# Feature-major tiles with each low-weight product between two high-weight ones

## The chip, the cores and the metric

The kernel runs on one core of one Trainium2 chip. The time is the device time of one execution in microseconds; before the change the median of 3 runs is 2253.44 us (2252.5 to 2256.35). The engines of the core work side by side: TensorE multiplies matrices (PE in the profile, and PEld for the load of its stationary operand), VectorE (DVE) and ScalarE (ACT) do elementwise work, SyncE (SP) issues the transfers.

## The reference

Two transformer blocks follow one another over 256 tokens of width 2048, all in float32. Nearly all of the arithmetic is in products of the activations with weight matrices: an input projection, an output projection, an up-projection and a down-projection in each block.

```python
h = rms_norm(x, pre_mix_norm[l])
proj = h @ w_in[l]                      # queries, keys, values, gates
...
x = x + rms_norm(mix @ w_out[l], post_mix_norm[l])
h = rms_norm(x, pre_ffn_norm[l])
u = causal_dwconv(h @ w_up[l], conv_w[l], conv_b[l])
gate, up = jnp.split(u, 2, axis=-1)
y = (jax.nn.gelu(gate, approximate=True) * up) @ w_down[l]
x = x + rms_norm(y, post_ffn_norm[l])
```

The second block has the same frame with another attention, a recurrent branch and an up-projection without the convolution.

## The kernel before

**Weights.** Every weight matrix passes through the core once, in tiles of 128 x 1024 float32 (512 KB). SyncE loads them into eight slots of `stage`. ScalarE copies a tile to `whi` in the matmul's reduced float32 format (L786 for the up-projections), and VectorE writes what that copy lost, stage - whi, to `wlo` (L1220). Both have four slots (`SPLITS`). The activations are kept in the same way: in `actT[:, k, :]` columns 0 to 255 hold the high parts of 256 tokens for chunk k of 128 input features, and columns 256 to 511 the low parts. A product in float32 is then hi x hi + lo x hi + hi x lo, three products in the reduced format.

**Feature-major tiles** give an output with features on the partitions: the weights are the stationary operand, the activations stream. A tile holds 4 chunks (`FC`) of 256 features, in two halves f = 0, 1 of 128. For a chunk and a half there is one high-weight product, whi against all 512 columns, into the whole of PSUM bank f, and one low-weight product, wlo against the 256 high columns, added to columns 256 to 511 of the same bank. So a chunk has the high products of both halves and then the low products of both halves. Four tiles of 4 chunks run over the 2048 input features and fill two banks. Such tiles stand in three places with the same body: `feat` for the up-projections (L2018, L2022, in a loop on the engine), `in1_tile` for the first block's input projection (L2090, L2093), and `in2_tile` for the second's (L2361, L2364).

**Token-major tiles** (`tok`, `tok_tile`) have the activations as stationary operand and stream the weights, 512 columns wide in most, 256 or 280 in a few; three products a chunk and half of the tokens (L1905 to L1907; L2106 to L2108; L2374 to L2376). They aren't touched.

**What sets the order.** TensorE's program is written out by hand and runs in that order. At its first load a tile waits for `lo_done` (VectorE has written its wlo), and its last product increments `tile_used`. ScalarE waits for that before it writes over the slot of four tiles ago. SyncE refills a `stage` slot once VectorE has read it. In the first block after a norm (`turned`), each chunk also waits for `actlo_...`, its activations' low part.

Of the kernel before, what the change touches and what calls it, by code (L numbers as in the profile page):

```python
# [16 lines left out]
P = 128  # L17
D = 2048
S = 256
TT = S // P  # L20
KC = D // P
# [29 lines left out]
SPLITS = 4  # L51
# [4 lines left out]
FW = 256  # L56
FC = TILE // FW
FT = 2 * KC // FC
# [50 lines left out]
def in1_block(n):  # L109

    k = max(k for k in range(len(IN1_BLOCKS)) if IN1_FIRST[k] <= n)
    return k, n - IN1_FIRST[k]
# [13 lines left out]
def in2_block(n):  # L126

    k = max(k for k in range(len(IN2_BLOCKS)) if IN2_FIRST[k] <= n)
    return k, n - IN2_FIRST[k]
# [74 lines left out]
def build(nc, w, out, scratch, roots):  # L204
# [4 lines left out]
    def ev(name):  # L209

        if name not in sems:
            sems[name] = ctx.enter_context(nc.semaphore(name))
        return sems[name]

    with ctx:
        def sb(name, shape, dt=F32, on=ctx):
            return on.enter_context(nc.sbuf_tensor(name, shape, dt))
# [3 lines left out]
        whi = sb("whi", [P, SPLITS, TILE], F32R)  # L221
        wlo = sb("wlo", [P, SPLITS, TILE], F32R)
# [15 lines left out]
        actT = sb("actT", [P, KC, 2 * S], F32R, here)  # L238
# [88 lines left out]
        PS = ctx.enter_context(nc.psum_tensor("PS", [P, 8, 512], F32))  # L327
# [1572 lines left out]
        def _(pe):  # L1900
# [47 lines left out]
            def last_chunks(turn):  # L1948

                n = {"n2": 0, "n3": 1, "n4": 2}[turn]  # L1950
                pe.wait_ge(ev("actlo_" + turn), 4)
                turn_chunks(turn, range(12, KC))
                pe.wait_ge(ev("resid"), PIECES * n + 6)
                turn_chunks(turn, range(12, KC), t=1)
# [43 lines left out]
            def feat(name, down=None, turned=None):  # L1998

                g = G[name]  # L2000

                def one(i, s):
                    new = turned is not None and isinstance(i, int) and i == 0
                    pe.wait_ge(ev("pre_done"), i + (g.acc + 1))
                    if s == 1 and down is not None:
                        pe.wait_ge(ev("acc_free"), 2 + G[down].acc + G[down].blocks)
                    for j in range(FT):
                        if new and j == 1:
                            last_chunks(turned)
                        pe.wait_ge(ev("lo_done"), i * FT + (g.first + j + 1 + STAGES))  # L2010
                        for c in range(FC):
                            k = j % (FT // 2) * FC + c
                            if new and j < FT // 2:
                                pe.wait_ge(ev("actlo_" + turned), k + 1)
                            for f in range(2):
                                o = PS[:, 4 * (s ^ g.turned) + 2 * (j // (FT // 2)) + f, :]
                                at = slice(c * FW + f * P, c * FW + (f + 1) * P)
                                nc.tensor.matmul(o, whi[:, j % SPLITS, at], actT[:, k, :], start=k == 0, stop=False)  # L2018
                            for f in range(2):
                                o = PS[:, 4 * (s ^ g.turned) + 2 * (j // (FT // 2)) + f, :]  # L2020
                                at = slice(c * FW + f * P, c * FW + (f + 1) * P)
                                last = nc.tensor.matmul(o[:, S:2 * S], wlo[:, j % SPLITS, at], actT[:, k, 0:S],  # L2022
                                                        start=False, stop=k == KC - 1)
                        last.then_inc(ev("tile_used"), 1)
                if turned is not None:
                    one(0, 0)
                    one(1, 1)
                with pe.Fori(1 if turned is not None else 0, g.blocks // 2) as r:
                    for s in range(2):
                        one(r * 2 + s, s)  # L2030

            def turn(name, ready, n):

# [38 lines left out]
            def in1_tile(n):  # L2072

                k, j = in1_block(n)
                kind, _, wd = IN1_BLOCKS[k]
                bank, s = 2 * (k % 2), n % SPLITS
                if k == 0:
                    pe.wait_ge(ev("actlo_n1"), FC * (j + 1))
                elif j == 0 and k >= 2:
                    if k - 2 in IN1_FEAT:  # L2080
                        pe.wait_ge(ev("in1_join"), IN1_FEAT[k - 2] + 1)
                    else:
                        pe.wait_ge(ev("in1_tok"), 2 * IN1_TOK[k - 2] + 2)
                pe.wait_ge(ev("lo_done"), n + 1 + STAGES)
                if kind == "feat":
                    for c in range(FC):
                        at_k = FC * j + c
                        for f in range(2):
                            o, at = PS[:, bank + f, :], slice(c * FW + f * P, c * FW + (f + 1) * P)
                            nc.tensor.matmul(o, whi[:, s, at], actT[:, at_k, :], start=at_k == 0, stop=False)  # L2090
                        for f in range(2):
                            o, at = PS[:, bank + f, :], slice(c * FW + f * P, c * FW + (f + 1) * P)
                            last = nc.tensor.matmul(o[:, S:2 * S], wlo[:, s, at], actT[:, at_k, 0:S], start=False, stop=at_k == KC - 1)  # L2093
                else:
                    last = tok_tile(bank, s, wd, TC * j)
                last.then_inc(ev("tile_used"), 1)
# [240 lines left out]
            def in2_tile(n):  # L2337

                k, j = in2_block(n)
                kind, _, wd = IN2_BLOCKS[k]  # L2340
                banks, s = IN2_BANKS[k], n % SPLITS
                if j == 0 and k == 14:
                    pe.wait_ge(ev("in2_join"), FEAT_NO[12] + 1)
                elif j == 0 and k > 14:
                    pe.wait_ge(ev("in2_tok"), 2 * TOK_NO[k - 2] + 2)
                elif k < 14 and j == 0 and k >= 2:
                    if k - 2 in FEAT_NO:
                        pe.wait_ge(ev("in2_join"), FEAT_NO[k - 2] + 1)
                    else:
                        pe.wait_ge(ev("in2_tok"), 2 * TOK_NO[k - 2] + 2)  # L2350
                if k == 0 and j == 2:
                    last_chunks("n3")
                if k == 0:
                    pe.wait_ge(ev("actlo_n3"), TC * (j + 1))
                pe.wait_ge(ev("lo_done"), G["in2"].first + n + 1 + STAGES)
                if kind == "feat":
                    for c in range(FC):
                        at_k = FC * j + c
                        for f in range(2):
                            o, at = PS[:, banks[f], :], slice(c * FW + f * P, c * FW + (f + 1) * P)  # L2360
                            nc.tensor.matmul(o, whi[:, s, at], actT[:, at_k, :], start=at_k == 0, stop=False)  # L2361
                        for f in range(2):
                            o, at = PS[:, banks[f], :], slice(c * FW + f * P, c * FW + (f + 1) * P)
                            last = nc.tensor.matmul(o[:, S:2 * S], wlo[:, s, at], actT[:, at_k, 0:S], start=False, stop=at_k == KC - 1)  # L2364
                else:
                    for t in range(TT):
                        if t == 1 and j == 0 and k >= 14:
                            pe.wait_ge(ev("in2_tok"), 2 * TOK_NO[k - 1] + 1)
                        for c in range(TC):
                            at_k = TC * j + c  # L2370
                            h, l = whi[:, s, c * wd:(c + 1) * wd], wlo[:, s, c * wd:(c + 1) * wd]
                            o = PS[:, banks[t], 0:wd]
                            ah, al = actT[:, at_k, t * P:(t + 1) * P], actT[:, at_k, S + t * P:S + (t + 1) * P]
                            nc.tensor.matmul(o, ah, h, start=at_k == 0, stop=False)  # L2374
                            nc.tensor.matmul(o, ah, l, start=False, stop=False)  # L2375
                            last = nc.tensor.matmul(o, al, h, start=False, stop=at_k == KC - 1)  # L2376
                        if t == 0 and j == 7 and k >= 13:
                            last.then_inc(ev("first_half"), 1)
                last.then_inc(ev("tile_used"), 1)
# [183 lines left out]
```

## Time and profile before

| | |
|---|---|
| median of 3 runs | 2253.44 us (2252.5 to 2256.35) |
| profiled execution, first to last instruction | 2250.0 us |
| its own time beyond the span | not listed; the median of the runs is 3.44 us above the span |
| TensorE, matmuls | 2225.6 us, 99% |
| TensorE, weight loads | 1890.7 us, 84% |
| VectorE | 1415.9 us, 63% |
| ScalarE | 1117.9 us, 50% |
| mean HBM and DMA rate | 186 GB/s |

Matmuls are pipelined, and the end of each is modelled by the profiler, so a record is longer than the time until the next one starts, and records overlap. The busy time of TensorE therefore says only that it never stands still for long, not that it works at its peak.

### The profile page before, as it was taken

How to read it: one execution, taken by the hardware profiler on the slowest of the kernel's cores; microseconds unless marked ns; L12 is line 12 of the kernel's file. 1: busy time of each engine (PE TensorE's matmuls, PEld its weight loads, DVE VectorE, ACT ScalarE, POOL GpSimd, SP SyncE). 2: the span in 40 equal slices, each digit the busy share in tenths (PEclk: the TensorE clock that was granted, in tenths of full speed). 3: DMA queues.
4: the chain of work that ended last, by engine and by line, in shares of the span. 5: the costliest groups of instructions: out<-in, count | busy, mean ns of one | idle time of the engine just before them, and what ended most of it. 6: DMA issues, size and time to landing. Idle time of an engine off the chain costs nothing.

```text
span 2250.0 us, 34148 instructions
## 1 busy us (share of the span) xinstructions
PE 2225.6 (99%) x12721; PEld 1890.7 (84%) x12721; DVE 1415.9 (63%) x1826; ACT 1117.9 (50%) x1566; POOL 65.6 (3%) x95
## 2 busy tenths in 40 slices
PE   8999999999999999999999999999999999999998
PEld 7888888888888888888888888888888888888886
DVE  5567685677776447777566786656665444666545
ACT  5454464555555445555454554545444344444443
POOL 4100000000000000000000000000000000000000
PEclk9999999999999999999999999999999999999999
DMA  9954455566566666656657455566666666666663
GB/s 286 312 182 135 132 168 178 157 192 204 177 199 193 189 193 188 186 187 199 205 147 204 141 165 156 181 194 170 189 193 189 191 191 190 192 187 189 213 188 111
DMA packets 321663, 418.84 MB, mean 186 GB/s; under 512 B 13566, under 2 KB 233048, under 8 KB 320788
## 3 DMA queue, kind: packets, MB, share of 16 engines
q1 hardware_dynamic: 316548, 398.81, 58.4%
q0 software_dynamic: 4720, 16.49, 2.5%
q10 hardware_dynamic: 288, 2.10, 0.2%
q8 instruction: 69, 1.13, 0.2%
q14 instruction: 38, 0.31, 0.0%
HBM read 414.85 MB, written 2.49 MB: 185 GB/s over the span
## 4 chain that ended last, share of the span: by engine, by line
PE 93%; DVE 3%; DMA 2%; ACT 1%; issue 1%; POOL 0%; SPq 0%; POOLq 0%; DVEq 0%; ACTq 0%
PE PS L2018 24%; PE PS L2022 12%; PE PS L1907 10%; PE PS L1906 10%; PE PS L1905 10%; PE PS L2090 5%; PE PS L2361 3%; PE PS L2093 2%; PE PS L2106 2%; PE PS L2108 2%; PE PS L2107 2%; PE PS L2364 2%; PE PS L2374 1%; PE PS L2376 1%; PE PS L2375 1%; DMA root_rows<-small 1%
## 5 line engine op out<-in xcount | busy, mean ns | idle before, releaser
L2018 PE MATMUL PS<-actT,whi 128*128 128x512 f32 x2432 | 759.1, 393 | 0.2 <-DVE wlo L1220 0.2
L2022 PEld LDWEIGHTS PS<-actT,wlo 128*128 128x128 f32 x2432 | 457.2, 188 | 103.5
L1220 DVE TENSOR_TENSOR wlo<-stage,whi 128x1024 fp32r<-128x1024 f32 x296 | 360.2, 1223 | 220.4 <-ACT whi L786 220.1
L1192 DVE TENSOR_TENSOR wlo<-stage,whi 128x1024 fp32r<-128x1024 f32 x245 | 299.1, 1226 | 307.3 <-ACT whi L728 307.3
L2022 PE MATMUL PS<-actT,wlo 128*128 128x256 f32 x2432 | 479.5, 279 | 0.0
L786 ACT ACTIVATE whi<-stage 128x1024 fp32r<-128x1024 f32 x296 | 311.6, 1058 | 308.1 <-PE PS L2022 294.6
L728 ACT ACTIVATE whi<-stage 128x1024 fp32r<-128x1024 f32 x245 | 258.6, 1058 | 351.1 <-PE PS L1907 327.5
L2018 PEld LDWEIGHTS PS<-actT,whi 128*128 128x128 f32 x2432 | 366.3, 188 | 0.9 <-issue 0.4
L1907 PE MATMUL PS<-whi,gT 128*128 128x512 f32 x864 | 340.4, 394 | 0.0
L1906 PE MATMUL PS<-wlo,gT 128*128 128x512 f32 x864 | 338.7, 392 | 0.0
L1905 PE MATMUL PS<-whi,gT 128*128 128x512 f32 x864 | 335.2, 388 | 0.0
L1623 DVE TENSOR_TENSOR wlo<-stage,whi 128x1024 fp32r<-128x1024 f32 (+2 forms) x125 | 145.4, 1166 | 110.0 <-ACT whi L977 109.7
L977 ACT ACTIVATE whi<-stage 128x1024 fp32r<-128x1024 f32 (+2 forms) x125 | 125.7, 1008 | 150.2 <-PE PS L2093 80.7
L1906 PEld LDWEIGHTS PS<-wlo,gT 128*128 128x128 f32 x864 | 162.2, 188 | 37.8
L1905 PEld LDWEIGHTS PS<-whi,gT 128*128 128x128 f32 x864 | 162.2, 188 | 36.1
L1907 PEld LDWEIGHTS PS<-whi,gT 128*128 128x128 f32 x864 | 162.4, 188 | 32.2
L2090 PE MATMUL PS<-actT,whi 128*128 128x512 f32 x512 | 163.5, 400 | 1.2 <-DVE wlo L1404 1.2
L1831 DVE TENSOR_TENSOR wlo<-stage,whi 128x1024 fp32r<-128x1024 f32 (+1 forms) x86 | 102.9, 1203 | 62.7 <-ACT whi L1128 62.2
L1128 ACT ACTIVATE whi<-stage 128x1024 fp32r<-128x1024 f32 (+1 forms) x86 | 89.3, 1044 | 90.2 <-PE PS L2364 45.3
L2361 PE MATMUL PS<-actT,whi 128*128 128x512 f32 x384 | 121.7, 398 | 0.7 <-DVE wlo L1831 0.7
L2093 PEld LDWEIGHTS PS<-actT,wlo 128*128 128x128 f32 x512 | 96.2, 188 | 22.0
L2093 PE MATMUL PS<-actT,wlo 128*128 128x256 f32 x512 | 101.1, 279 | 0.0
(334 smaller groups left out, 2479.3 us busy)
## 6 DMA issues: line engine op xcount, KB each, us to landing
stage<-in_w_up SPq DMA_DIRECT2D x304, 512.0 KB, 4.0
stage<-in_w_down SPq DMA_DIRECT2D x216, 512.0 KB, 4.2
stage<-in_w_in SPq DMA_DIRECT2D x160, 512.0 KB, 3.8
stage<-in_w_out SPq DMA_DIRECT2D x64, 512.0 KB, 4.1
stage<-in_w_in SPq DMA_DIRECT2D x16, 256.0 KB, 3.3
DQK<-in_cmp_k_w POOLq DMA_DIRECT2D x8, 512.0 KB, 7.4
DQK<-in_cmp_v_w POOLq DMA_DIRECT2D x8, 512.0 KB, 7.3
stage<-in_w_in SPq DMA_DIRECT2D x8, 280.0 KB, 8.1
```

The lines of the kernel that those rows point to most:

```text
L728: nc.scalar.activation(whi[:, s % SPLITS, 0:wd], stage[:, s % STAGES, 0:wd], ACT.Copy)\
L786: nc.scalar.activation(whi[:, j % SPLITS, :], stage[:, j, :], ACT.Copy).then_inc(ev("hi_done"), 1)
L1192: nc.vector.tensor_tensor(wlo[:, s % SPLITS, 0:wd], stage[:, s % STAGES, 0:wd], whi[:, s % SPLITS, 0:wd].bitcast(F32), ALU.subtract).then_ ...
L1220: nc.vector.tensor_tensor(wlo[:, j % SPLITS, :], stage[:, j, :], whi[:, j % SPLITS, :].bitcast(F32), ALU.subtract).then_inc(ev("lo_done"), 1)
L1905: nc.tensor.matmul(o, ah, h, start=k == 0, stop=False)
L1906: nc.tensor.matmul(o, ah, l, start=False, stop=False)
L1907: return nc.tensor.matmul(o, al, h, start=False, stop=ends and c == TC - 1)
L2018: nc.tensor.matmul(o, whi[:, j % SPLITS, at], actT[:, k, :], start=k == 0, stop=False)
L2022: last = nc.tensor.matmul(o[:, S:2 * S], wlo[:, j % SPLITS, at], actT[:, k, 0:S], start=False, stop=k == KC - 1)
L2090: nc.tensor.matmul(o, whi[:, s, at], actT[:, at_k, :], start=at_k == 0, stop=False)
L2093: last = nc.tensor.matmul(o[:, S:2 * S], wlo[:, s, at], actT[:, at_k, 0:S], start=False, stop=at_k == KC - 1)
L2361: nc.tensor.matmul(o, whi[:, s, at], actT[:, at_k, :], start=at_k == 0, stop=False)
```

## The change

The three bodies of a feature-major tile are replaced by one function, `feat_tile`. It issues the same sixteen products in another order: the low product of the second half is held back by one chunk and put between the two high products of the next chunk, and the low product of the first half follows the second high product. At the end of a tile the last low product that was held back is issued.

```diff
+            def feat_tile(bank, s, k0, before_chunk=None):
+
+                def high(f, c):
+                    at = slice(c * FW + f * P, c * FW + (f + 1) * P)
+                    nc.tensor.matmul(PS[:, bank + f, :], whi[:, s, at], actT[:, k0 + c, :], start=k0 + c == 0, stop=False)
+
+                def low(f, c):
+                    at = slice(c * FW + f * P, c * FW + (f + 1) * P)
+                    return nc.tensor.matmul(PS[:, bank + f, S:2 * S], wlo[:, s, at], actT[:, k0 + c, 0:S],
+                                            start=False, stop=k0 + c == KC - 1)
+
+                for c in range(FC):
+                    if before_chunk is not None:
+                        before_chunk(k0 + c)
+                    high(0, c)
+                    if c:
+                        low(1, c - 1)
+                    high(1, c)
+                    low(0, c)
+                return low(1, FC - 1)
...
                 if kind == "feat":
-                    for c in range(FC):
-                        at_k = FC * j + c
-                        for f in range(2):
-                            o, at = PS[:, bank + f, :], slice(c * FW + f * P, c * FW + (f + 1) * P)
-                            nc.tensor.matmul(o, whi[:, s, at], actT[:, at_k, :], start=at_k == 0, stop=False)
-                        for f in range(2):
-                            o, at = PS[:, bank + f, :], slice(c * FW + f * P, c * FW + (f + 1) * P)
-                            last = nc.tensor.matmul(o[:, S:2 * S], wlo[:, s, at], actT[:, at_k, 0:S], start=False, stop=at_k == KC - 1)
+                    last = feat_tile(bank, s, FC * j)
```

In `feat` and `in2_tile` the same body is replaced by the same call. In `feat` the wait for a chunk's activations is passed as `before_chunk`.

TensorE, one tile of the up-projections in the engine's loop, before. L2018 is a high product, L2022 a low one, and L2010 computes the value of the wait at a tile's start.

```order
L2010 REGISTER_ALU
L2018 MATMUL PS<-actT,whi 128x512 x2
L2022 MATMUL PS<-actT,wlo 128x256 x2
L2018 MATMUL PS<-actT,whi 128x512 x2
L2022 MATMUL PS<-actT,wlo 128x256 x2
L2018 MATMUL PS<-actT,whi 128x512 x2
L2022 MATMUL PS<-actT,wlo 128x256 x2
L2018 MATMUL PS<-actT,whi 128x512 x2
L2022 MATMUL PS<-actT,wlo 128x256 x2
L2010 REGISTER_ALU
```

The products stand in pairs of two highs and two lows. The same engine with the change, from the third chunk of such a tile over its end into the next one; L2028 is now the high product, L2032 the low one.

```order
L2028 MATMUL PS<-actT,whi 128x512
L2032 MATMUL PS<-actT,wlo 128x256
L2028 MATMUL PS<-actT,whi 128x512
L2032 MATMUL PS<-actT,wlo 128x256
L2028 MATMUL PS<-actT,whi 128x512
L2032 MATMUL PS<-actT,wlo 128x256 x2
L2010 REGISTER_ALU
L2028 MATMUL PS<-actT,whi 128x512 x2
L2032 MATMUL PS<-actT,wlo 128x256
L2028 MATMUL PS<-actT,whi 128x512
L2032 MATMUL PS<-actT,wlo 128x256
L2028 MATMUL PS<-actT,whi 128x512
```

Inside a tile high and low products take turns; one pair of lows is left at its end and one pair of highs at its start. The programs of the other engines have the same instructions in the same order as before.

## Rows read from the trace of the kernel before

**Rows 1.** The page: busy us (share) x instructions; clock in 40 slices; chain by engine.
```profile
PE 2225.6 (99%) x12721; PEld 1890.7 (84%) x12721; DVE 1415.9 (63%) x1826; ACT 1117.9 (50%) x1566; POOL 65.6 (3%) x95
...
PEclk9999999999999999999999999999999999999999
...
PE 93%; DVE 3%; DMA 2%; ACT 1%; issue 1%; POOL 0%; SPq 0%; POOLq 0%; DVEq 0%; ACTq 0%
```

**Rows 2.** The page's groups: shapes, count, busy us, mean ns, idle us before, its releaser.
```profile
L2018 PE MATMUL PS<-actT,whi 128*128 128x512 f32 x2432 | 759.1, 393 | 0.2 <-DVE wlo L1220 0.2
...
L786 ACT ACTIVATE whi<-stage 128x1024 fp32r<-128x1024 f32 x296 | 311.6, 1058 | 308.1 <-PE PS L2022 294.6
...
L2090 PE MATMUL PS<-actT,whi 128*128 128x512 f32 x512 | 163.5, 400 | 1.2 <-DVE wlo L1404 1.2
...
L2361 PE MATMUL PS<-actT,whi 128*128 128x512 f32 x384 | 121.7, 398 | 0.7 <-DVE wlo L1831 0.7
```

**Rows 3.** Stretches: length, busy us per engine, granted clock, DMA share, GB/s.
```profile
428.00:822.00 394.00, 393.85 (x2093) 338.00 (x2091) 258.17 (x300) 205.24 (x244) 3.38 (x4) 1.00 0.62 191
```

**Rows 4.** Timeline of TensorE, up-projection: start us, us; eight chunks apart.
```profile
1700.00 0.39 PE L2018 MATMUL PS<-actT,whi 128*128 128x512 f32 x1
...
1705.55 0.39 PE L2018 MATMUL PS<-actT,whi 128*128 128x512 f32 x1
```

**Rows 5.** Single products of one chunk, in order: min/median/max ns, first and last start.
```profile
L2018 PE MATMUL PS<-actT,whi x1: 388/388/388, 1700.0 to 1700.0; 128*128 128x512 f32 x1
...
L2018 PE MATMUL PS<-actT,whi x1: 398/398/398, 1700.2 to 1700.2; 128*128 128x512 f32 x1
...
L2022 PE MATMUL PS<-actT,wlo x1: 281/281/281, 1700.5 to 1700.5; 128*128 128x256 f32 x1
...
L2022 PE MATMUL PS<-actT,wlo x1: 276/276/276, 1700.6 to 1700.6; 128*128 128x256 f32 x1
```

**Rows 6.** Single products of a token-major chunk, same columns.
```profile
L1905 PE MATMUL PS<-whi,gT x1: 388/388/388, 700.0 to 700.0; 128*128 128x512 f32 x1
...
L1906 PE MATMUL PS<-wlo,gT x1: 392/392/392, 700.3 to 700.3; 128*128 128x512 f32 x1
...
L1907 PE MATMUL PS<-whi,gT x1: 394/394/394, 700.5 to 700.5; 128*128 128x512 f32 x1
```

**Rows 7.** Timeline of TensorE, token-major: five triples apart.
```profile
700.04 0.39 PE L1905 MATMUL PS<-whi,gT 128*128 128x512 f32 x1
...
703.47 0.39 PE L1905 MATMUL PS<-whi,gT 128*128 128x512 f32 x1
```

**Rows 8.** Waits of TensorE on its high products: us in total, times, longest.
```profile
PE PS L2018 <- DVE wlo L1220: 0.2, 1, 0.2
```

**Rows 9.** Single 512-column products: after 512; after 256 token-major; after a stall; after low.
```profile
L2018 PE MATMUL PS<-actT,whi x1: 394/394/394, 824.3 to 824.3; 128*128 128x512 f32 x1
...
L2361 PE MATMUL PS<-actT,whi x1: 394/394/394, 1174.9 to 1174.9; 128*128 128x512 f32 x1
...
L2107 PE MATMUL PS<-wlo,actT x1: 396/396/396, 171.2 to 171.2; 128*128 128x512 f32 x1
...
L1905 PE MATMUL PS<-whi,gT x1: 390/390/390, 692.5 to 692.5; 128*128 128x512 f32 x1
```

**Rows 10.** Groups of 256-column token-major products, 66 to 70 and 73 to 77 us.
```profile
L2108 PE MATMUL PS<-whi,actT 128*128 128x256 f32 x13 | 3.6, 276 | 0.0
...
L2106 PE MATMUL PS<-whi,actT 128*128 128x256 f32 x12 | 3.4, 280 | 0.0
L2108 PE MATMUL PS<-whi,actT 128*128 128x256 f32 x12 | 3.3, 279 | 0.0
L2107 PE MATMUL PS<-wlo,actT 128*128 128x256 f32 x12 | 3.3, 279 | 0.0
```

**Rows 11.** Weight loads of the high products, 1700 to 1800 us: min/median/max ns.
```profile
L2018 PEld LDWEIGHTS PS<-actT,whi x36: 187/188/188, 1699.9 to 1711.8; 128*128 128x128 f32 x36
```

More of the change, by code:

```diff
@@ L2010, in one, with chunk_split @@
                         pe.wait_ge(ev("lo_done"), i * FT + (g.first + j + 1 + STAGES))
-                        for c in range(FC):
-                            k = j % (FT // 2) * FC + c
+                        def chunk_split(k):
                             if new and j < FT // 2:
                                 pe.wait_ge(ev("actlo_" + turned), k + 1)
-                            for f in range(2):
-                                o = PS[:, 4 * (s ^ g.turned) + 2 * (j // (FT // 2)) + f, :]
-                                at = slice(c * FW + f * P, c * FW + (f + 1) * P)
-                                nc.tensor.matmul(o, whi[:, j % SPLITS, at], actT[:, k, :], start=k == 0, stop=False)
-                            for f in range(2):
[L2020 to L2024, printed above, removed]
+                        feat_tile(4 * (s ^ g.turned) + 2 * (j // (FT // 2)), j % SPLITS, j % (FT // 2) * FC, chunk_split)\
+                            .then_inc(ev("tile_used"), 1)
                 if turned is not None:
@@ L2085, in in1_tile @@
                 if kind == "feat":
-                    for c in range(FC):
-                        at_k = FC * j + c
-                        for f in range(2):
-                            o, at = PS[:, bank + f, :], slice(c * FW + f * P, c * FW + (f + 1) * P)
-                            nc.tensor.matmul(o, whi[:, s, at], actT[:, at_k, :], start=at_k == 0, stop=False)
-                        for f in range(2):
-                            o, at = PS[:, bank + f, :], slice(c * FW + f * P, c * FW + (f + 1) * P)
-                            last = nc.tensor.matmul(o[:, S:2 * S], wlo[:, s, at], actT[:, at_k, 0:S], start=False, stop=at_k == KC - 1)
+                    last = feat_tile(bank, s, FC * j)
                 else:
@@ L2356, in in2_tile @@
                 if kind == "feat":
[L2357 to L2364, printed above, removed]
+                    last = feat_tile(banks[0], s, FC * j)
                 else:
```

## Prediction

> **What bounds the kernel now.** I read the page first. TensorE is busy for 99% of the span, its clock row stands at 9 in every slice, and the chain of waits lies on it for 93% [rows 1]. VectorE and ScalarE, which cut the weight tiles into a high and a low part, spend their idle time waiting for TensorE to free a slot (ScalarE's whi copy of L786: 308.1 us idle, 294.6 of it released by L2022) [rows 2]. In the stretch that holds the first up-projection, 428 to 822 us, the DMA engines are used to 0.62 and TensorE is busy for 393.85 of 394 us [rows 3]. So no transfer and no other engine is near the path there: what a chunk of matmuls costs TensorE is what the kernel costs.
>
> Then I went down to single instructions. Feature-major tiles have 2432 + 512 + 384 high-weight products (L2018, L2090, L2361) [rows 2]. A tile has eight, so there are 3328 / 8 = 416 tiles, of 4 chunks of two high (512 columns) and two low (256 columns). In the timeline the first high product of a chunk starts at 1700.00 and the same one eight chunks on at 1705.55 [rows 4]: 5.55 / 8 = 694 ns a chunk, 2.775 us a tile, and 416 tiles x 2.775 = 1154 us, half of the kernel. At the full clock (granted 1.00 in rows 3, the 2.4 GHz level) 1536 columns would stream in 640 ns. 54 ns a chunk, 416 x 4 x 54 = 90 us in all, are thus not column time. They are all that an order of the same sixteen matmuls can win back.
>
> Recorded durations tell how far one start lies from the next. The four of a chunk last 388, 398, 281 and 276 ns [rows 5]; their sum is 1343, the pitch 694, so each record is (1343 - 694) / 4 = 162 ns longer than its pitch. Token-major tiles confirm the 162: 388 + 392 + 394 = 1174 [rows 6] against five triples from 700.04 to 703.47, 686 ns each [rows 7]; (1174 - 686) / 3 = 163. I therefore use differences of records as differences of pitch. What the reader should see in rows 5 is that the two high products of a chunk differ by 10 ns, and the two low ones by 5, although the two are the same instruction with another bank and other weights.
>
> **What the change does.** It adds and removes no instruction. Per tile there are again 8 high and 8 low products, as many weight loads, one wait for lo_done at the tile's first load and one increment at its last product; banks, slots and SP's and the converters' programs stay. What moves is the neighbourhood. Before, each chunk was H H L L, so of eight highs four came after a low and four after a high. Now a tile is H H L H L H L H L H L H L H L L. Of the highs one is first (after the last tile's low, before a high), one second (after a high, before a low), and six stand between two lows; of the lows six stand between two highs, and the last two are as before. At a tile's end the product whose end frees the slot is still the last one, so nobody gets a buffer earlier or later within a tile. In the first blocks after a norm, a chunk's wait for its activations (actlo) now also stands ahead of the last low product of the chunk before. That concerns 16 chunks of two calls, and TensorE's waits list only 0.2 us at L2018 [rows 8]; I take it as nothing, and if each such product stood exposed it would be 30 x 0.12 = 3.6 us.
>
> The whole effect is therefore the price of a high between lows and of a low between highs. The trace of before has neither. I bound them by the nearest rows: the high at 388 or 398, the low at 276 or 281 [rows 5]. Both at the low end give 6 x (393 - 388) + 6 x (278.5 - 276) = 45 ns a tile below before (a tile's averages are 393 and 278.5), 416 x 0.045 = 18.7 us; both at the high end give 18.7 us more.
>
> Which end depends on what makes rows 5 differ, the product ahead or the one behind.
> If it is the **product ahead** (the state in which it leaves the array and the load path), a high after a low costs 388 and a low after a high 281. Per tile: 6 x (388 - 393) = -30, 6 x (281 - 278.5) = +15, sum -15 ns. 416 x -0.015 = -6.2 us.
> For it: a high after a high, with a high behind it too, is found once at the border from a token-major block, 394 [rows 9]; with a low ahead the same product is 388 [rows 5]. So 6 of the 10 ns come with the product ahead. The second product after a stall has no low near it, and reads 396 [rows 9].
> Against it: a high after a token-major low-width product reads 394 [rows 9], not 388, and the 256-column products of token-major tiles run at 276 in one stretch and at 279 to 280 in another, with the same neighbours [rows 10]. So more than the neighbour counts.
>
> I take -6.2 us, because three of the four comparisons that rows 9 allow go with the product ahead or do not speak against it (the fourth: a token-major high after a low is 390, within the 388 to 394 of its kind [rows 6, 9]).
>
> Here a rule of the Trainium skill speaks against the change. The load of a low product's successor has only the low product to hide under: load records last 188 ns and begin with the matmul ahead [rows 11], while a low product's pitch is 276 - 162 = 114 to 119 ns. "TensorE: Matmul & The Clock Gate", section "LDWEIGHTS (loading the stationary operand)", says that a load takes its columns divided by 1.2 GHz, an estimate of 107 ns for 128 columns, and its part 2 that loads are pulled ahead under the running matmul. By that there is one load under every product in either order, and the sum would be nothing, 2253.4 us.
>
> **Rivals.**
> B, the **costs add up, whatever the order**. In token-major tiles a high averages (388 + 392 + 394) / 3 = 391.3, and a 256-column product at its slower pitch 279.3 [rows 6, 10]; 2 x 391.3 + 2 x 279.3 = 1341 against the 1343 of a chunk. Or, read in two parts, 6 ns of a high come from ahead and 4 from behind (388, 394, 398), so a high between lows is 392, and a low 276 to 281: per tile 6 x (392 - 393) + 6 x (-2.5 to +2.5) = -21 to +9 ns, -8.7 to +3.7 us, middle -2.5, time 2250.9 us. For it: the sum fits to 2 ns. Against it: such a fit is no proof while 256-column products have two pitches.
>
> C, **slower: the product behind sets the pitch**, because its weights load during it. A high with a low behind it then costs 398, a low with a high behind it 276. Per tile 6 x (398 - 393) + 6 x (276 - 278.5) = +15 ns, 416 x 0.015 = +6.2 us, time 2259.6 us. The place is each of the six inner high products of every tile, and it decides once more than half of the 10 ns in rows 5 is owed to the wlo load that follows. For it: the rows 5 that carry A carry C equally well, as ahead and behind change together there. Against it: the 394 and 396 of rows 9, slow highs with no low behind them.
>
> That the change does nothing that it says is excluded by the order of the program: the rows of the section on the change show each low product between two high ones.
>
> **The numbers.** The profiled execution has a span of 2250.0 us, and the median of the runs is 3.4 above it; the difference lies outside the span and is left as it is. 2253.44 - 6.2 = 2247.2 us. About 0.2%, 4.5 us, is what a measurement of this kernel can tell from no change. A has 0.42, and would be seen as faster. B has 0.33: 0.05 faster, 0.25 same, 0.03 slower. C has 0.25: 0.22 slower, 0.03 same. Faster 0.47, same 0.28, slower 0.25. The range goes from 2240 (between A and the bound of -18.7) to 2261 (C with the small waits of the first blocks partly exposed); beyond it at either end lies a tenth. A's own range is 2241 (inner highs at 388 and inner lows at their old average: 30 ns a tile, -12.5 us) to 2250.
>
> **What would show it.** For A: in the profile after, eight chunks of an inner stretch take about 5.52 us instead of 5.55 (15 ns a tile), the inner highs read 388 and the inner lows 281, the share of DMA rises by less than 0.01 and the waits stay as they are. For B: highs near 392 and lows near 278. For C: highs at 398, lows at 276. All fail if the inner pair falls into a rhythm of its own, below 276 or above 398, or if a wait for wlo appears at the tile starts. Token-major tiles must stay at 388, 392, 394; if they move, something outside these tiles is at work.

## The result and the profile after

The changed kernel takes 2270.15 us (median of 4 runs, 2269.3 to 2270.91) against 2253.43 us (4 runs): ratio 1.0075, 95% interval 1.0057 to 1.0093. It is slower by 16.7 us where 6.2 us faster was forecast, and lies above the range's upper end of 2261.

One correction to the time before: each run lists its span beside its time, and the time is 1.8 us longer (2270.44 against 2268.6 us here, 2251.94 against 2250.1 us in a run of the kernel before). So of the 3.44 us that the section on the time before puts beyond the span, some 1.6 us are that its three runs were slower than the profiled execution. That is also most of why the medians differ by 16.7 us and the spans by 18.6.

The page and a stretch of 400 us from the first up-projection into the down-projection behind it:

```profile
span 2268.6 us, 34148 instructions
...
PE 2244.2 (99%) x12721; PEld 1899.7 (84%) x12721; DVE 1416.8 (62%) x1826; ACT 1119.4 (49%) x1566; POOL 65.8 (3%) x95
...
L2028 PE MATMUL PS<-actT,whi 128*128 128x512 f32 x3328 | 1148.1, 398 | 1.9 <-DVE wlo L1404 1.3
L2032 PE MATMUL PS<-actT,wlo 128*128 128x256 f32 x3328 | 867.7, 281 | 0.0
...
L786 ACT ACTIVATE whi<-stage 128x1024 fp32r<-128x1024 f32 x296 | 312.9, 1058 | 322.4 <-PE PS L2032 308.9
```

```profile
432.00:832.00 400.00, 400.00 (x2099) 341.61 (x2098) 258.93 (x300) 207.17 (x245) 3.39 (x4) 1.00 0.62 189
```

Counts, clock and DMA share are those of before [rows 1 to 3], no new wait has come up (1.9 us in all at L2028, as much as at the three lines before), and ScalarE idles 14 us longer for TensorE [rows 2]. The span has grown by 18.6 us, on TensorE. L2028 and L2032 now stand for all three places. The mean record of a high product there is 398 ns; before, the three lines give (2432 x 393 + 512 x 400 + 384 x 398) / 3328 = 395 [rows 2]. A low one reads 281 on average, and 279 before. So the time is in the pitch of the moved products, that is, in the time from one start to the next. The timeline from the inside of one tile to the end of the next (start us, us):

```profile
1709.99 0.40 PE L2028 MATMUL PS<-actT,whi 128*128 128x512 f32 x1
1710.22 0.28 PE L2032 MATMUL PS<-actT,wlo 128*128 128x256 f32 x1
1710.34 0.40 PE L2028 MATMUL PS<-actT,whi 128*128 128x512 f32 x1
1710.58 0.28 PE L2032 MATMUL PS<-actT,wlo 128*128 128x256 f32 x1
1710.69 0.40 PE L2028 MATMUL PS<-actT,whi 128*128 128x512 f32 x1
1710.93 0.40 PE L2032 MATMUL PS<-actT,wlo 128*128 128x256 f32 x2
1711.17 0.39 PE L2028 MATMUL PS<-actT,whi 128*128 128x512 f32 x1
...
1713.99 0.63 PE L2028 MATMUL PS<-actT,whi 128*128 128x512 f32 x2
```

A pair of high and low takes 0.35 us (1709.99, 1710.34, 1710.69), and a tile 1713.99 - 1711.17 = 2.82 us. Over forty tiles the starts are

```profile
1926.45 0.63 PE L2028 MATMUL PS<-actT,whi 128*128 128x512 f32 x2
...
2039.25 0.63 PE L2028 MATMUL PS<-actT,whi 128*128 128x512 f32 x2
```

so 112.80 / 40 = 2.820 us a tile. Before, the same forty tiles start at

```profile
1910.46 0.62 PE L2018 MATMUL PS<-actT,whi 128*128 128x512 f32 x2
...
2021.40 0.62 PE L2018 MATMUL PS<-actT,whi 128*128 128x512 f32 x2
```

and take 110.94 / 40 = 2.773 us each. 416 tiles x 0.0467 = 19.4 us, slightly more than the span's 18.6: not every tile runs at the steady pitch, and in the first up-projection forty tiles of the kernel before take 2.784 us each. The single records (min/median/max ns) that answer to rows 5:

```profile
L2028 PE MATMUL PS<-actT,whi x1: 398/398/398, 1710.0 to 1710.0; 128*128 128x512 f32 x1
...
L2032 PE MATMUL PS<-actT,wlo x1: 281/281/281, 1710.2 to 1710.2; 128*128 128x256 f32 x1
...
L2028 PE MATMUL PS<-actT,whi x1: 394/394/394, 1708.3 to 1708.3; 128*128 128x512 f32 x1
```

Between two lows the high reads 397 to 398 (but for the first of the six in a tile, 392), between two highs the low reads 281 to 283: each takes the dearer of its two values in rows 5. A pair is (398 - 162) + (281 - 162), nearly 354 ns; from the forty tiles' starts it is 353.3, against 346.7 as the mean of before. The two highs at a tile's start, 394 each (the last row), add up to 788 ns, where 388 and 398 were 786.

### The profile page after: what moved, and what is told of

Same layout as the page of the kernel before. It is cut to its first block, busy times and chain, and to the rows that moved or that the text cites. A ratio compares the mean times of both kernels' runs of the same rounds, so it can differ in the third digit from the quotient of the medians.

```text
span 2268.6 us, 34148 instructions
## 1 busy us (share of the span) xinstructions
PE 2244.2 (99%) x12721; PEld 1899.7 (84%) x12721; DVE 1416.8 (62%) x1826; ACT 1119.4 (49%) x1566; POOL 65.8 (3%) x95
## 4 chain that ended last, share of the span: by engine, by line
PE 95%; DVE 2%; DMA 1%; ACT 1%; issue 1%; POOL 0%; SPq 0%; POOLq 0%; DVEq 0%; ACTq 0%
PE PS L2028 33%; PE PS L2032 17%; PE PS L1906 10%; PE PS L1905 10%; PE PS L1907 10%; PE PS L2112 2%; PE PS L2114 2%; PE PS L2113 2%; PE PS L2373 1%; PE PS L2375 1%; PE PS L2374 1%; DVE x L1354 1%; DMA root_rows<-small 1%; PE PS L2143 0%; PE PS L2236 0%
## 5 line engine op out<-in xcount | busy, mean ns | idle before, releaser
L2028 PE MATMUL PS<-actT,whi 128*128 128x512 f32 x3328 | 1148.1, 398 | 1.9 <-DVE wlo L1404 1.3
L2032 PE MATMUL PS<-actT,wlo 128*128 128x256 f32 x3328 | 867.7, 281 | 0.0
L2028 PEld LDWEIGHTS PS<-actT,whi 128*128 128x128 f32 x3328 | 596.2, 188 | 123.1 <-issue 6.1
L2032 PEld LDWEIGHTS PS<-actT,wlo 128*128 128x128 f32 x3328 | 624.6, 188 | 37.9
L1220 DVE TENSOR_TENSOR wlo<-stage,whi 128x1024 fp32r<-128x1024 f32 x296 | 360.5, 1224 | 234.7 <-ACT whi L786 234.4
L1906 PE MATMUL PS<-wlo,gT 128*128 128x512 f32 x864 | 340.4, 394 | 0.0
L1905 PE MATMUL PS<-whi,gT 128*128 128x512 f32 x864 | 338.7, 392 | 0.0
L1907 PE MATMUL PS<-whi,gT 128*128 128x512 f32 x864 | 335.3, 388 | 0.0
L1905 PEld LDWEIGHTS PS<-whi,gT 128*128 128x128 f32 x864 | 162.2, 188 | 37.8
L1907 PEld LDWEIGHTS PS<-whi,gT 128*128 128x128 f32 x864 | 162.2, 188 | 36.3
L1906 PEld LDWEIGHTS PS<-wlo,gT 128*128 128x128 f32 x864 | 162.4, 188 | 32.1
L1243 DVE SCALAR_TENSOR_TENSOR grow<-pre,convT,grow 128x256 f32<-128x256 f32 x176 | 73.6, 481 | 31.7 <-ACT grow L801 29.0
L2112 PE MATMUL PS<-whi,actT 128*128 128x512 f32 (+2 forms) x240 | 88.9, 371 | 0.0
L2114 PE MATMUL PS<-whi,actT 128*128 128x512 f32 (+2 forms) x240 | 87.1, 363 | 0.0
L2113 PE MATMUL PS<-wlo,actT 128*128 128x512 f32 (+2 forms) x240 | 86.8, 362 | 0.0
```

The source lines that it names most:

```text
L1220: nc.vector.tensor_tensor(wlo[:, j % SPLITS, :], stage[:, j, :], whi[:, j % SPLITS, :].bitcast(F32), ALU.subtract).then_inc(ev("lo_done"), 1)
L1905: nc.tensor.matmul(o, ah, h, start=k == 0, stop=False)
L1907: return nc.tensor.matmul(o, al, h, start=False, stop=ends and c == TC - 1)
L2028: nc.tensor.matmul(PS[:, bank + f, :], whi[:, s, at], actT[:, k0 + c, :], start=k0 + c == 0, stop=False)
L2032: return nc.tensor.matmul(PS[:, bank + f, S:2 * S], wlo[:, s, at], actT[:, k0 + c, 0:S], start=False, stop=k0 + c == KC - 1)
```

## The experiments

All numbers of tile pitch below are from starts some 32 to 40 tiles apart in one up-projection. Each run's ratio is to runs of the kernel before on the same chip (medians of 2251.9 to 2255.0 us). First, which neighbourhood costs: four other orders of the same sixteen products, and later e7, a fifth. In the expectations of e1 to e4, rival B is the bank and rival C the chunk; they aren't the rivals B and C of the prediction.

```diff
 e1: per chunk        high(0, c); low(0, c); high(1, c); low(1, c)
 e2: per chunk        high(0, c); low(0, c - 1); high(1, c); low(1, c - 1); two lows at the end
 e3: per two chunks   four highs, then four lows
 e4: per tile         eight highs (0, 1, 0, 1, ...), then eight lows
 e7: per tile         high(0, 0..3), high(1, 0..3), then the lows likewise
```

> Order H0 L0 H1 L1 of the same chunk: widths alternate as in the changed kernel, but a low product follows the high one of its own bank and of its own chunk, and the next high goes to the other bank. Theory W (a product costs more when its neighbours have the other width; 15 ns of TensorE time for each pair of changes high-low and low-high, from 45 ns a tile for three more such pairs): 8 pairs a tile where before had 4, so 60 ns a tile over before, 416 x 0.060 = 25 us, about 2278 us; inner highs recorded at 397, lows at 281. Rival B (the high that follows a low writes into the bank that the low has just written): that is gone here, 2253 us. Rival C (the stream changes its chunk of activations at nearly every product): half gone here, about 2262 us.

> Both low products stand one chunk behind: H0(c) L0(c-1) H1(c) L1(c-1). Banks as in e1 (a low follows a high of the same bank, the next high changes bank), but every product streams another chunk than the one ahead of it. Theory W: a tile is H0 H1 first, then alternates, and ends on two lows, as in the changed kernel, 7 pairs, about 2270 us. Rival B (bank of the next high): 2253 us. Rival C (chunk changes at each product): 2270 us or more, and clearly above e1.

> Two chunks at a time: four highs, then four lows. Theory W: 2 pairs of width changes a tile instead of 4, 30 ns a tile less than before, 416 x 0.030 = 12.5 us, about 2241 us. Rivals B and C: the banks change at each product as before, and the chunk changes no more often: 2253 us. If a high costs 229 and a low 118 wherever neighbours are equal (the token-major rates), the four cost 693 a chunk as before: 2253 us too.

> The whole tile at a time: eight highs, then eight lows. Theory W: 1 pair of width changes a tile instead of 4, 45 ns a tile less than before, 18.7 us, about 2235 us. Rivals B and C, and flat token-major rates (229 and 118): 2253 us. If the lows in a row fall into their faster rhythm (276 recorded, 114 pitch), 8 x 4 = 32 ns a tile or 13 us less even under flat rates: 2240 us; the recorded durations tell the two apart (highs at 388 to 391 and lows at 276 to 278, against highs at 391 and lows at 276).

e1 took 2272.1 us (ratio 1.0088, 1.0072 to 1.0105), tile 2.827 us. That is eight pairs of 353.3 ns, with none of the tile's ends in another order. e2 took 2276.7 us (1.0110, 1.0093 to 1.0127), although its tile is shorter, 2.807 us. e3 took 2252.0 us (1.0001, 0.9991 to 1.0010) and e4 2252.2 us (1.0001, 0.9991 to 1.0010); the tile of both is 2.773 us, to the nanosecond that of before.

Bank (B) and chunk (C) are out: e1 and e2 have other banks behind the low, e1 also the same chunk twice, and in neither is an alternating pair cheaper. e2's tile is 13 ns shorter than the changed kernel's because fewer of its products alternate (three highs in a row at its start, three lows at its end); that e2 takes longer in spite of it has another cause, shown below. Theory W, a price for each change of width, is out as well: with 4, 2 or 1 pairs of changes a tile the pitch is the same. Here is e4's tile (start us, us):

```profile
1706.74 2.02 PE L2028 MATMUL PS<-actT,whi 128*128 128x512 f32 x8
1708.60 1.07 PE L2032 MATMUL PS<-actT,wlo 128*128 128x256 f32 x8
1709.51 0.85 PE L2028 MATMUL PS<-actT,whi 128*128 128x512 f32 x3
```

Eight highs take 1.86 us, 232.5 each, and eight lows 0.91, 114 each. So lows in a row are cheap and highs in a row not cheaper than before. Of the orders tried only strict alternation costs, and it costs 353.3 ns a pair in all of them. e4's expectation for lows at 276 was met by the records and missed in time, since the highs gave it back.

> The tile as eight highs and then eight lows as in e4, but sorted by bank: four highs into one bank, four into the other, then the lows likewise. In e4 the highs ran at 231 and 236 ns in turn, the banks in turn too, and moving columns shared by each two. Theory K (a change of bank, or of the stream, costs 5 ns): with one bank kept, three of four highs cost 226 to 229 instead of 233 on average, 6 x 5 = 30 ns a tile, 12 us, about 2240 us. Rival: which bank is written doesn't matter, and 2252 us as e4.

e7 took 2253.3 us (0.9995, 0.9986 to 1.0005), tile 2.773 us: sorting the highs by bank changes nothing.

Next, what alternation lacks. Under a low of 256 columns lies the load of the next high. e5 and e6 make the low 384 columns wide, e12 and e15 320.

```diff
-                    return nc.tensor.matmul(PS[:, bank + f, S:2 * S], wlo[:, s, at], actT[:, k0 + c, 0:S],
+                    return nc.tensor.matmul(PS[:, bank + f, 0:384], wlo[:, s, at], actT[:, k0 + c, 0:384],
```

> The order of the kernel before, with each low product 384 columns wide instead of 256 (it adds the low weights also to the left half's sum and, for 128 tokens, the product of low with low). The control for e6. A product of N columns took N / 2.4 plus 10 to 16 ns so far, so the low costs about 160 + 13 = 173 ns instead of 116: 2 x 57 ns a chunk, 1664 chunks, +190 us, about 2443 us. All theories expect the same.

> The order of the changed kernel with low products 384 columns wide. Theory U (the weight load of the next high doesn't fit under a low product of 256 columns, and two lows in a row are needed to make up for it; 384 columns cover it): no difference from e5, within 5 us. Theory W (a neighbour of another width costs, whatever covers it): again 45 ns a tile, 19 us over e5, high products recorded near 397 between lows.

e5 took 2454.5 us and e6 2448.5 us (ratios 1.0880, 1.0861 to 1.0898, and 1.0859, 1.0841 to 1.0877). At 384 columns alternation is no longer slower. By the medians it is 6 us ahead, just beyond the 5 us that theory U allowed; the two intervals overlap, and one of e5's four runs took 2449.6, so the tiles below are the better evidence. W wanted it 19 us behind. e5 itself was expected at 2443: its lows are 177 ns apart, not 173, for the 10 to 16 ns over N / 2.4 were read too narrowly (the records of rows 5, less 162 ns, give 7 to 23). From 1800 to 1810 us, e5 and then e6 (count, busy us, mean ns):

```profile
L2028 PE MATMUL PS<-actT,whi 128*128 128x512 f32 x26 | 8.2, 394 | 0.0
L2032 PE MATMUL PS<-actT,wlo 128*128 128x384 f32 x24 | 6.2, 338 | 0.0
```

```profile
L2028 PE MATMUL PS<-actT,whi 128*128 128x512 f32 x25 | 9.3, 392 | 0.0
L2032 PE MATMUL PS<-actT,wlo 128*128 128x384 f32 x26 | 8.3, 338 | 0.0
```

The lows cost the same in both orders, and the highs are 2 ns cheaper where they alternate. Tiles: 3.280 us in e5, 3.260 in e6.

> The changed kernel with low products 320 columns wide (adding products of low with low for 64 tokens). 320 columns stream in 133 ns. A pair of high and low without any loss against two highs and two lows costs 231 + 133 + 13 = 377 to 380 ns. Theory U, with a load that needs no more than 133 ns: 377 to 380 ns or less and thus about 2253 + 3328 x 0.031 = 2356 us, highs recorded below 397. If the load needs longer than 133 ns, the pair is near 388 and the time near 2375 us.

> The order of the kernel before with low products 320 columns wide, the control for e12 (2357.4 us, of which some 9 us are 698 token-major triples at 700 ns). If a low of 320 columns covers the load of the next high, both orders have the same tile pitch, 3.00 to 3.02 us, and this one is at 2348 us if its triples stay at 687. If the old order is still the better one at 320 columns, its tile is at 2.97 us or below (2 x 231 + 2 x 140 = 742 ns a chunk) and the time at 2335 us.

e12 took 2357.4 us (1.0458, 1.0441 to 1.0476). Its pair, 3.013 / 8 = 377 ns, is what theory U put; that the time fits to 1 us is partly luck, since 9 us of it are slow token-major blocks that the expectation didn't have. e15, its control, took 2359.3 us (1.0478, 1.0461 to 1.0496) and met neither of its cases. Its tile is 3.040 us, e12's 3.013 on average, so at 320 columns too the alternating order has the shorter tile, by 27 ns. In time most of that is lost to slower token-major blocks, of which below.

Then the load itself. With half of the weight columns a load is shorter, while the streamed columns and the order are unchanged. (The product then also writes only 64 of its 128 output rows; no run here separates the two.) e8 asks whether it matters where the low weights lie.

```diff
 e9 and e11 (high), e10 (low, in the same way), chunks 1 and 2 of each tile:
+                    n = 64 if c in (1, 2) else P
+                    at = slice(c * FW + f * P, c * FW + f * P + n)
-                    nc.tensor.matmul(PS[:, bank + f, :], whi[:, s, at], ...
+                    nc.tensor.matmul(PS[0:n, bank + f, :], whi[:, s, at], ...
 e8, the low product:
-                    return nc.tensor.matmul(PS[:, bank + f, S:2 * S], wlo[:, s, at], ...
+                    return nc.tensor.matmul(PS[:, bank + f, S:2 * S], whi[:, s, at], ...
```

> The changed kernel with the low product's weights taken from whi instead of wlo (so the low part of the weights is left out, and the high part counted twice for half the columns). If alternating between two weight buffers (their place in memory) makes the pair 353 ns, it falls to 347 or less and the time to 2253 us or below. Theories U and W expect 2270 us as for the changed kernel.

One run, 2270.4 us, tile 2.820: the buffer has no part in it.

> The changed kernel, in which the high products of chunks 1 and 2 of each tile load only 64 of 128 weight columns (half of their outputs is left out); columns streamed and order stay. Four of the seven low products that have a high behind them then have half a load to cover. Theory U (the load of the next high is what a 256-column low can't cover): those four pairs fall from 353 ns to 347 or less, at least 4 x 6.7 = 27 ns a tile, 11 us, so 2259 us or less; if they fall to 340, 2248. Theory H (not the load, but the rhythm of a high and a low stream itself): 2270 us.

> The changed kernel with half loads for the low products of chunks 1 and 2 instead (half of the low part is left out there). These loads run under highs of 512 columns. Theory U: no gain, 2270 us, inner lows still recorded at 281. Rival L (the load of the low weights delays the high above it, hence its 235 instead of 226): the highs ahead of these lows fall toward 226, up to 4 x 9 = 36 ns a tile, 15 us, 2255 us.

> The kernel before with the same half loads of high weights as e9, its control. A chunk's second low covers half a load for two chunks a tile, and its first high covers half a load. Theory U: little to gain, since two lows in a row already make up for the load: 2249 to 2253 us. If half loads speed up anything else, it shows here as much as in e9.

e9 took 2259.4 us (1.0033, 1.0021 to 1.0046): 10.7 us less than the changed kernel, 9.5 by the two ratios. The loads and the products of e9 from 1700 to 1715 us:

```profile
L2030 PEld LDWEIGHTS PS<-actT,whi 128*128 128x128 f32 x21 | 3.6, 188 | 0.4
L2030 PEld LDWEIGHTS PS<-actT,whi 128*64 128x64 f32 x22 | 2.9, 134 | 0.9
```

```profile
L2034 PE MATMUL PS<-actT,wlo 128*128 128x256 f32 x43 | 11.2, 280 | 0.0
L2030 PE MATMUL PS<-actT,whi 128*64 128x512 f32 x22 | 7.9, 391 | 0.0
L2030 PE MATMUL PS<-actT,whi 128*128 128x512 f32 x22 | 7.5, 396 | 0.0
```

A load is 54 ns shorter, and the high that it is for reads 391; the highs in the changed kernel read 396 on average (1700 to 1714 us). The tile is 2.793 us, 26.7 ns less, so 6.7 ns for each of the four pairs. By the records some 20 of the 26.7 ns are saved in the four narrowed highs themselves, the rest in the lows. A difference of 54 ns for 64 columns also agrees with the Trainium skill ("TensorE: Matmul & The Clock Gate", "LDWEIGHTS (loading the stationary operand)": a load takes its columns / 1.2 GHz, from which 53 ns is an estimate).

e10 took 2267.1 us (1.0066, 1.0050 to 1.0083), tile 2.813: one step of 6.7 ns a tile for four halved loads of low weights, which U had put at nothing and L at 36 ns. e11 took 2252.4 us (1.0003, 0.9993 to 1.0013), tile 2.773: halving the same loads as e9 in the old order gains nothing, as U put it.

So e9, e11, e6 and e12 all point to the load that lies under the low product as what costs in alternation. They don't prove it: e10 gained a little where U had nothing, and in e9 the narrower product could have its part beside the shorter load. Nor is the load simply too long for 256 columns, since in e4 such lows with full loads follow each other at 114 ns, and in the old order the second low of a chunk has a high's load beneath it and costs 114 too.

The last question came from e2, slower than its tiles allow. (2.807 - 2.773) x 416 = 14 us; it lost 25. Its token-major products, whose code is untouched, on the page:

```profile
L1905 PE MATMUL PS<-whi,gT 128*128 128x512 f32 x864 | 343.4, 397 | 0.0
L1906 PE MATMUL PS<-wlo,gT 128*128 128x512 f32 x864 | 343.4, 397 | 0.0
L1907 PE MATMUL PS<-whi,gT 128*128 128x512 f32 x864 | 343.3, 397 | 0.0
```

Before, these were 388, 392 and 394 [rows 6] in every block. Now 854 of their 1001 triples that nothing interrupts take 700 ns instead of 687, 11.4 us. e13 and e14 swap the order in one tile of four, the last ahead of each change of bank and so ahead of each token-major block:

```diff
+                if k0 + FC == KC:   # e13: e2's order here and the old one elsewhere; e14: the old one here, e2's elsewhere
```

> The order of the kernel before in three of four tiles, the order of e2 in the last tile of each four (so in the last tile ahead of each token-major block). Theory R (the pitch of a token-major block is that in which the stream enters it, and it keeps it): the triples after an up-projection run at 700 instead of 687 ns as in e2, 854 x 13.3 = 11.4 us, plus a quarter of e2's own 34 ns a tile, 416 x 0.034 / 4 = 3.5 us; 2252 + 15 = 2267 us. If the rhythm of token-major blocks in e2 had another reason: 2255 to 2256 us, triples at 687.

> The converse: e2's order in three of four tiles, the order of the kernel before in the last tile of each four. Theory R: token-major triples are back at 687 ns, 11.4 us less than e2, and a quarter of the tiles cost 34 ns less, 3.5 us: 2276.7 - 15 = 2262 us. Otherwise: 2273 us.

e13 took 2268.7 us (1.0073, 1.0056 to 1.0090), e14 2263.8 us (1.0051, 1.0034 to 1.0068). The token-major products from 740 to 760 us, e13:

```profile
L1905 PE MATMUL PS<-whi,gT 128*128 128x512 f32 x29 | 11.5, 397 | 0.0
L1906 PE MATMUL PS<-wlo,gT 128*128 128x512 f32 x29 | 11.5, 397 | 0.0
L1907 PE MATMUL PS<-whi,gT 128*128 128x512 f32 x29 | 11.5, 397 | 0.0
```

and e14:

```profile
L1907 PE MATMUL PS<-whi,gT 128*128 128x512 f32 x30 | 11.8, 394 | 0.0
L1906 PE MATMUL PS<-wlo,gT 128*128 128x512 f32 x30 | 11.8, 392 | 0.0
L1905 PE MATMUL PS<-whi,gT 128*128 128x512 f32 x29 | 11.3, 388 | 0.0
```

Both are within 2 us of what theory R put. Between e13 and e14 the order of the tiles ahead decides in what rhythm the next 110 to 180 us of other code run: in e13, 855 triples take 700 ns; in e14 none stay there. e2 leaves its last tile with three lows (698 us; min/median/max ns), e14 with two:

```profile
L2032 PE MATMUL PS<-actT,wlo x3: 280/281/281, 697.9 to 698.2; 128*128 128x256 f32 x3
```

```profile
L2032 PE MATMUL PS<-actT,wlo x2: 277/279/281, 698.0 to 698.1; 128*128 128x256 f32 x2
```

The rhythm of 687 is lost where the last low reads 281 and kept where it reads 277. But the changed kernel and e1 leave with 281 too and yet keep 687, so that record alone doesn't decide. Nor does the order ahead: in e12 every last tile has the same order, and three of its four long blocks run at 700 and one at 687. Here are the products of two of them, from 740 to 760 us and from 1120 to 1140 us:

```profile
L1905 PE MATMUL PS<-whi,gT 128*128 128x512 f32 x29 | 11.5, 397 | 0.0
...
L1905 PE MATMUL PS<-whi,gT 128*128 128x512 f32 x30 | 11.8, 392 | 0.0
```

The two are entered from different places in the tile's own rhythm: the last high ahead of the first reads 388, ahead of the second 394. One of e12's four runs took 2350.6 us, 7 us less than the others; it has no trace, so whether its blocks fell otherwise is open. What decides is not shown.

The times of the runs with 256-column lows follow within 3 us from two numbers, the tile's pitch and the token-major triples. The sums start from the median of the kernel before in the same comparison:

| kernel | tile, us | 416 x (tile - 2.7733) | slow triples x 13.3 ns | sum | measured |
|---|---|---|---|---|---|
| changed | 2.8200 | 19.4 | 0 | 2272.8 | 2270.2 |
| e1 | 2.8267 | 22.2 | 0 | 2274.2 | 2272.1 |
| e2 | 2.8067 | 13.9 | 11.4 | 2277.3 | 2276.7 |
| e3, e4, e7, e11 | 2.7733 | 0 | 0 | 2252.0, 2252.0, 2255.0, 2251.9 | 2252.0, 2252.2, 2253.3, 2252.4 |
| e9 | 2.7933 | 8.3 | 0 | 2260.2 | 2259.4 |
| e10 | 2.8133 | 16.6 | 0 | 2268.5 | 2267.1 |
| e13 | 2.7867 (mean of four) | 5.5 | 11.4 | 2269.1 | 2268.7 |
| e14 | 2.8033 (mean of four) | 12.5 | 0 | 2264.6 | 2263.8 |

With wider lows the same sum comes out too high, by 4 us for e12 and e15 and by 9 to 11 us for e6 and e5.

No order tried beats the kernel before at 256 columns.

## Why the prediction was wrong, step by step

**What bounds the kernel** held. TensorE's pitch is the time, no wait came or went, and the loss is, to 3 us, 416 tiles times what a tile lost. Two side readings were wrong and changed nothing: the 3.4 us beyond the span are 1.8 (see above), and VectorE's idle time at L1220 ends with ScalarE's copy, not with TensorE.

**The bounds** held only just. The step named the high at 388 or 398 and the low at 276 or 281, and +18.7 us with both at the high end. That end is what happened: 397 to 398 and 281, +19.4 us by the tiles, +16.7 in the median.

**The step that failed** is the one right behind it: "Which end depends on what makes rows 5 differ, the product ahead or the one behind." It assumed that one neighbour sets the pitch, so that one of the two prices must go down when the other goes up. The forecast of -6.2 and rival C's +6.2 both rest on it, and the case in which both go up got no chance, although its 18.7 us stood in the text; the range ended at 2261, 9 us short of the result. The runs put a property of the whole stream in its place: in strict alternation at 256 columns, a pair takes 353.3 ns whatever the bank, chunk or buffer (e1, e2, e8), against 346.7 on average with two or more lows in a row (before, e3, e4). Narrower weights for the highs bring the pair back to 346.7 (e9), narrower ones for the lows gain a quarter of that (e10), and with wider lows alternation is the cheaper order (e6, e12). One sign of failure in the prediction did name the right thing, an inner pair that "falls into a rhythm of its own", but placed it outside 276 to 398, where it wasn't.

**Rows 9 were misread.** They were counted as votes for a neighbour's effect. With the 394 behind a token-major low and the two pitches of 256-column products [rows 10] they fit the other reading better, that a stream keeps a rhythm it has come into. The text said "more than the neighbour counts" and then did not price it.

**Rival A** was wrong for highs (397, not 388) and right for lows (281). **Rival C** was right for highs and wrong for lows (281, not 276). **Rival B**, a fixed price whatever the order, holds for e3, e4 and e7 and fails for the change itself. That groupings of two, four and eight cost the same is what its fixed prices say; they leave out only alternation.

**The rule of the Trainium skill** (the same page and section), by which the prediction had one load under every product in either order and hence no difference, gave 2253.4 us and was 17 us off. What 64 columns more add to a load agrees with it (e9). Whether a load hides depends on more than its length.

**The small parts**: the first blocks' waits at nothing were right (1.9 us listed at all feature-major highs; before, 0.2 + 1.2 + 0.7 at the three lines in rows 2), and token-major tiles kept their three values 388, 392 and 394 in the changed kernel, if not in e2. (The values moved on by one product: L1905 reads 392, L1906 394 and L1907 388. They belong to a place in the rhythm, not to a line of code.)

What stays open: whether it is the load alone that costs in alternation, why two lows in a row escape the price of the load beneath them, and which entry puts a token-major block into 700 ns.

## What to carry to other kernels

When short and long matmuls with fresh weights mix, their order can cost time though counts and columns stay the same, so time a few groupings. Here strict alternation was the worst at 256 columns and the better one at 320 and 384, and narrower weights for the long products removed its price. When a trace shows one instruction at two pitches with the same neighbours, treat the pitch as a state of the stream, and keep both ends of the bound for all of its products at once in the range. And after such an edit look at the untouched code behind it, since it can have changed its pitch too.

## What the runs showed of the hardware

TensorE's stream has rhythms that it keeps. A token-major triple takes 687 or 700 ns for whole blocks of 110 to 180 us at a granted clock of 0.998 to 0.999, depending on how the stream enters the block (e13 against e14, and e12, which has both). Nearly all steady pitches are whole multiples of 6.67 ns: the tiles of 2773.3, 2793.3, 2806.7, 2813.3, 2820.0, 2826.7, 3040, 3260 and 3280 ns are 416, 419, 421, 422, 423, 424, 456, 489 and 492 of them, and the triples 103 and 105; each of the four half loads in e9 took one off. Which of two orders of the same products is faster depends on their width: alternation is 47 ns a tile behind at 256 columns, 27 ns ahead at 320 and 20 ns ahead at 384.
